# Modulation weights as the moving side, four 32-column tiles at a time, in a two-layer block chain

## The reference, cut to what matters

```python
def ada_mod(cond, w, b, n):
    m = jax.nn.silu(cond) @ w[:, :n * D_MODEL] + b[:n * D_MODEL]
    return m.reshape(m.shape[:-1] + (n, D_MODEL))
...
    for l in range(DEPTH):
        ml = ada_mod(c, w_ada[l], b_ada[l], N_MOD)[:, None]
        mc = ada_mod(c_ctx, w_ada[l], b_ada[l], 2 if last else N_MOD)

        hl = modulate(x, ml[..., 0, :], ml[..., 1, :])
        hc = modulate(ctx, mc[0], mc[1])
        zl = hl @ w_in[l] + b_in[l]
...
        x = layer_norm(DEEPNORM_ALPHA * x + ml[..., 2, :] * mix(zl, attn_l), ln1_g[l], ln1_b[l])

        x = layer_norm(DEEPNORM_ALPHA * x + ml[..., 5, :] * ffn(modulate(x, ml[..., 3, :], ml[..., 4, :])),
                       ln2_g[l], ln2_b[l])
```

## Time and profile before

| | us |
|---|---|
| median of 3 runs | 3683.21 |
| lowest, highest | 3680.97, 3690.7 |
| profiled execution | 3681.75 |
| its span, first to last instruction | 3680.0 |

### The profile page before, as it was taken

One profiled execution on the slowest core, in us unless ns is written; L12 is line 12 of the kernel. 1 busy time (PEld: TensorE's weight loads), 2 busy tenths in 40 slices (PEclk: granted clock), 3 DMA queues, 4 the chain that ended last, 5 costly groups with the idle time before them and its releaser, 6 DMA issues.

```text
span 3680.0 us, 46744 instructions
## 1 busy us (share of the span) xinstructions
PE 3446.7 (94%) x17080; PEld 2772.8 (75%) x17080; DVE 1949.7 (53%) x2633; ACT 1258.7 (34%) x1750; POOL 848.1 (23%) x336
## 2 busy tenths in 40 slices
PE   8999979999979999997999999889997999999997
PEld 8899866787858888875887777678884875677665
DVE  2678886622446253446767873474554624244233
ACT  1221235224233222224223534243224345453433
POOL 1000200232213223230012033334442321332211
PEclk9999999999989999998999999999998989999899
DMA  5333100112102111213531023222221210221111
GB/s 209 125 137 120 51 20 8 50 50 78 62 29 69 63 63 62 64 57 115 173 107 46 7 74 104 85 74 92 96 94 59 69 52 29 75 86 46 63 35 58
DMA packets 72807, 272.00 MB, mean 74 GB/s; under 512 B 8528, under 2 KB 9040, under 8 KB 71888
## 3 DMA queue, kind: packets, MB, share of 16 engines
q1 hardware_dynamic: 71216, 256.04, 21.2%
q10 hardware_dynamic: 1440, 13.89, 1.0%
HBM read 264.66 MB, written 5.24 MB: 73 GB/s over the span
## 4 chain that ended last, share of the span: by engine, by line
PE 86%; DVE 6%; ACT 3%; issue 2%; DVEq 1%; ACTq 1%; DMA 1%; SPq 0%
PE ps L497 47%; PE ps L733 10%; PE ps L589 5%; PE ps L467 4%; PE ps L504 3%; PE ps L567 2%; PE ps L682 2%; PE ps L869 1%; PE ps L555 1%; PE ps L846 1%; PE ps L704 1%; PE ps L967 1%; PE ps L948 1%; PE ps L840 1%; PE ps L964 1%
## 5 line engine op out<-in xcount | busy, mean ns | idle before, releaser
L429 POOL TENSOR_TENSOR w_lo<-w_raw,w_hi 128x1024 fp32r<-128x1024 f32 x332 | 847.9, 2556 | 2792.5 <-ACT w_hi L1064 2792.4
L497 PE MATMUL ps<-act_hi,w_hi 128*128 128x512 f32 x2656 | 570.9, 363 | 9.3 <-DVE arena L2016 2.0
L497 PE MATMUL ps<-act_lo,w_hi 128*128 128x512 f32 x2656 | 560.9, 357 | 0.0
L497 PE MATMUL ps<-act_hi,w_lo 128*128 128x512 f32 x2656 | 547.4, 354 | 0.0
L497 PEld LDWEIGHTS ps<-act_hi,w_hi 128*128 128x128 f32 x2656 | 440.9, 190 | 96.8 <-issue 22.4
L1064 ACT ACTIVATE w_hi<-w_raw 128x1024 fp32r<-128x1024 f32 x380 | 399.8, 1054 | 294.0 <-PE ps L497 89.7
L497 PEld LDWEIGHTS ps<-act_hi,w_lo 128*128 128x128 f32 x2656 | 434.7, 188 | 72.0
L497 PEld LDWEIGHTS ps<-act_lo,w_hi 128*128 128x128 f32 x2656 | 433.0, 188 | 67.8
L1858 DVE SCALAR_TENSOR_TENSOR x<-arena,vec,x 128x512 f32<-128x512 f32 x336 | 220.2, 684 | 0.0
L1850 DVE SCALAR_TENSOR_TENSOR arena<-arena,vec 128x783 f32<-128x783 f32 (+1 forms) x240 | 219.8, 916 | 0.0
L589 PEld LDWEIGHTS ps<-cond,arena 128*128 128x128 f32 x1152 | 163.4, 217 | 18.2 <-issue 11.1
(11 more groups left out here) (309 smaller groups left out, 4967.4 us busy)
## 6 DMA issues: line engine op xcount, KB each, us to landing
w_raw<-in_weights SPq DMA_DIRECT2D x380, 512.0 KB, 3.4
arena<-in_ada_w SPq DMA_DIRECT2D x72, 512.0 KB, 4.5
tmp<-in_ada_w SPq DMA_DIRECT2D x24, 512.0 KB, 4.9
x<-in_x SPq DMA_DIRECT2D x1, 3072.0 KB, 13.6
x<-in_x ACTq DMA_DIRECT2D x1, 3072.0 KB, 9.9
x_mid<-x ACTq DMA_DIRECT2D x1, 3072.0 KB, 9.7
x<-x_mid ACTq DMA_DIRECT2D x1, 3072.0 KB, 10.0
arena<-in_pool_w ACTq DMA_DIRECT2D x2, 1024.0 KB, 5.0
```

Source lines behind the costliest of these rows:

```text
L429: nc.gpsimd.tensor_tensor(WL[:, w], raw, WH[:, w].bitcast(f32), ALU.subtract).then_inc(units_split, 1)
L497: last = nc.tensor.matmul(ps(t, a, b), w[:, s * UNIT + k * P:s * UNIT + (k + 1) * P], act[:, k * TOK + a:k * TOK + b], start=(n == 0 and k ...
```

## The change

The two sides of the modulation matmul are exchanged. The condition, after Silu, is written 16 times over into the space of `gla_w` (32 columns per chunk: 16 copies of 2), and is the stationary side; the weights move past it, 512 columns at a time. A step takes one chunk of 128 contracted channels and 2048 outputs (two slots of 512 KB) and is four matmuls, each writing another 32 partitions of one PSUM bank. Eight steps make the sums of two modulation vectors for both conditions, so the 96 units are 48 steps in 6 groups. A group's sums lie as rows: ACT copies them to the arena (`ada_copy`), and four float32 matmuls against columns of the identity turn them back into the columns that `modulation` reads (`ada_turned`).

- The first 8 steps have arena space of their own for 12 of their 16 loads, so SP issues all 16 without a wait; `x` comes behind them, in two halves. PE waits for `loaded`, the second half of `x` included, ahead of the first `ada_turned`.
- The other 40 steps stand ahead of whole units (`ada_ahead`), never in `first_pair` and no longer between the products of a unit: two ahead of the third unit of layer 0 and one ahead of each later one up to the end of `gate0`; in layer 1 one ahead of every second unit of `conv`, then one ahead of each, and two at the end.
- The loops of PE and ACT over these stages are written out. SP loads `gla_w` behind the last step.
- `TAPS_AT`, layer 0: per pair of units 14 -> 10, per gate 8 -> 6, per key head 3, per query head 3 -> 6, behind all heads 20 -> 10, per tile 1. Layer 1: 11 -> 8, 7 -> 5, key 1 -> 2, query 1 -> 5, behind 25 -> 14, per tile 2. The rest in `gate2` now stands ahead of the wait for the gate's tile.

```diff
-TAPS_AT = ((14, 8, 3, 20, 1), (11, 7, 1, 25, 2))
+TAPS_AT = ((10, 6, 3, 6, 10, 1), (8, 5, 2, 5, 14, 2))
...
-    STAGES += [((_l, "ada_rest"), 0, (0, 0, 0, 1)), ((_l, "conv"), 4, (8, 8, 0, 0)), ((_l, "gate0"), 2, (4, 4, 0, 0)),
+    STAGES += [((_l, "ada_rest"), 0, (0, 0, 1, 1)), ((_l, "conv"), 4, (8, 8, 0, 0)), ((_l, "gate0"), 2, (4, 4, 0, 0)),
...
-ADA_LATER = ((0, "conv", 4, (1, 0, 1)), (0, "gate0", 2, (1, 0, 1)), (1, "conv", 4, (0, 0, 1)), (1, "gate0", 2, (0, 1, 1)))
+ADA_LATER = ((0, "conv", 4, 2), (0, "gate0", 2, 2), (1, "conv", 4, 1), (1, "gate0", 2, 2))
+ADA_STEPS = CH
+ADA_AT = ({u: (0, 1) if u == 2 else (u - 1,) for u in range(2, 3 * CH + 1)},
+          {**{2 * i + 3: (24 + i,) for i in range(CH)}, **{u: (14 + u,) for u in range(18, 24)}, 24: (38, 39)})
+ADA_TURNED = ({9: 1, 17: 2, 25: 3}, {18: 4, 25: 5})
...
+            for i in range(ADA_FIRST // 2):
+                ada_early_load(i)
+            for dst, src in ((VEC1T, vec1_d), (IDENT, consts_d[0]), (PERM, consts_d[1]), (ONES, consts_d[2])):
                 sp.dma_start(dst[:, :], src).then_inc(loaded, 16)
             sp.dma_start(RC[:, :], consts_d[3][:, 0:64]).then_inc(loaded, 16)
+            for i in range(ADA_FIRST // 2, ADA_FIRST):
+                ada_early_load(i)
             for s in range(2):
                 sp.dma_start(RAW[:, s * UNIT:(s + 1) * UNIT], weights[s]).then_inc(raw_landed[s], 16)
-            with sp.Fori(1, ADA_FIRST // ADA_SLOTS) as r:
-                for s in range(ADA_SLOTS):
-                    sp.wait_ge(on(0, "ada_used"), r * ADA_SLOTS + (s - ADA_SLOTS + 1))
-                    ada_load(r * ADA_SLOTS + s, s)
+            for k, landed in enumerate((x_half, loaded)):
+                part = slice(k * CH // 2 * TOK, (k + 1) * CH // 2 * TOK)
+                sp.dma_start(X[:, part], x_d[:, part]).then_inc(landed, 16)
...
                 def single(i, s):
+                    if ahead:
+                        ahead(i * SLOTS + s)
                     start(i, s)
...
-            def ada_chunk(col, slot, k):
-                last = nc.tensor.matmul(at(PS, col + ADA_PS, 2), ada_slot(slot, k * P, P), COND[:, 2 * k:2 * k + 2],
-                                        start=(k == 0), stop=(k == CH - 1))
...
+            def ada_step(p, k, parts):
+
+                for m, src in enumerate(parts):
+                    for half in range(2):
+                        j = 2 * m + half
+                        last = nc.tensor.matmul(ada_sums(p, slice(32 * j, 32 * j + 32)),
+                                                GLA_W[:, 32 * k:32 * k + 32],
+                                                src[:, half * 512:half * 512 + 512], start=(k == 0), stop=(k == CH - 1))
+                last.then_inc(on(0, "ada_used"), 1)
+
+            def ada_turned(p):
+
+                pe.wait_ge(on(0, "ada_copied"), p + 1)
+                a = ADA_PS + mod(p // 3, p % 3 * 2, 0, 0)
+                for q in range(4):
+                    last = nc.tensor.matmul(PS[:, a:a + 4 * CH].rearrange("p (j q r) -> p q j r", j=4, q=4)[:, q:q + 1]
+                                            .rearrange("p q j r -> p (q j) r"),
+                                            AR[:, ADA_ROWS + q * P:ADA_ROWS + (q + 1) * P],
+                                            IDENT[:, :].rearrange("p (j x) -> p j x", j=4)[:, :, 0:2], start=True, stop=True)
+                last.then_inc(on(0, "ada_image"), 1)
...
                 if l == 0:
 
                     pe.wait_ge(*at_least(0, "cond", 1))
+                    pe.wait_ge(tile_free[2], taken(0, "ada_rest", 2, 0))
+                    for k in range(CH):
+                        pe.wait_ge(ada_landed[k // 2], 64)
+                        ada_step(0, k, [ada_early(2 * k), ada_early(2 * k + 1)])
+                    pe.wait_ge(loaded, 6 * 16)
                     pe.wait_ge(tile_free[3], taken(0, "ada", 3, 0))
+                    ada_turned(0)
...
+            def ada_copy(p, last):
+                act.wait_ge(on(0, "ada_used"), ADA_STEPS * (p + 1))
+                if p:
+                    act.wait_ge(on(0, "ada_image"), p)
+                i_ = nc.scalar.activation(AR[:, ADA_ROWS:ADA_ROWS + 512], ada_sums(p), ACT.Copy)
```

More of the change, by code:

```diff
@@ L389, in _ @@
                 sp.dma_start(INVF[:, :], consts_d[3][:, 64:65]).then_inc(tables_loaded, 16)
-            first = ADA_FIRST
-            for l, st, rounds, each in ADA_LATER:
-                n = sum(each)
+            first = 0
+            for l, st, rounds, n in ADA_LATER:
                 if l and st == "conv":
@@ L484, in linear @@
                                 single(j + 1, s)
+                elif ahead:
+                    for i in range(rounds):
+                        for s in range(SLOTS):
+                            single(i, s)
                 else:
@@ new lines, in block1 @@
+                    for c in range(CH):
+                        if c == CH // 2:
+                            act.wait_ge(loaded, 6 * 16)
+                        for j, (a, b) in enumerate(BOTH):
+                            last = nc.scalar.activation(XH[:, c * TOK + a:c * TOK + b], X[:, c * TOK + a:c * TOK + b], ACT.Identity,
+                                                        bias=at(MOD, mod(0, 0, c, j), 1), scale=at(MOD, mod(0, 1, c, j), 1))
+                        last.then_inc(on(l, "h_hi"), 1)
@@ L1230, in block1 @@
+                for j in range(CH):
+                    act.wait_ge(*at_least(l, "glu", j + 1))
+                    evacuate_unit(l, "gate0", j // SLOTS, j % SLOTS, AR[:, B0 + j * TOK:B0 + j * TOK + W], ACT.Sigmoid, B_MERGE)
+                    ada_behind(2 * CH + j)
                 act.wait_ge(*at_least(l, "qk_bias", 1))
```

143 lines of the change are left out of this document (68 added, 75 removed).

## The result

| | before | after |
|---|---|---|
| median | 3682.09 us (4 runs) | 3559.87 us (4 runs) |
| lowest, highest | 3677.12, 3690.7 | 3555.82, 3562.77 |
| profiled execution | 3681.75 | 3559.22 |
| its span | 3680.0 | 3557.4 |

A forecast was written before the change was run, and what follows sets the result against it. PE, holding 86% of the chain, was taken as the bound. Terms -35.6 (start and first pair), -42.4 and -35.1 (units), +0.9 (turn) and +2 (taps) gave -110: from 3681.75 to 3572 us, range 3555 to 3625.

The forecast's parts named there:

- Price of a step: One modulation step on PE: 0.85 us streaming plus 0.44 for entering and leaving tiled form, 1.3 us against 3.4.
- The row I went by: Profiled burst of 16 float32 matmuls on four 64 x 64 tiles, costing 1.29 us, taken as a step's price.
- a sharing of lanes: Rival, chance 0.19: column tiles share, a step takes 2.15 to 2.56 us, total 3606 to 3622 us.
- a line: Rival, chance 0.07: column tiles run one after another, a step takes 3.85 us, total 3702 us, slower.
- The start: Opening modulation, eight steps: loads and x set the time, first activation at 38 instead of 64.54 us, 26.5 earlier.
- First pair: First pair of layer 0, no modulation between products: 24.3 us instead of 33.4, 9.1 less.
- I let it cover three chunks again: First pair, layer 0: PE's slow pace lasts three chunks of 4.0 us, then five take 2.17 each.
- 22 units, layer 0: Layer 0 units behind the first pair, with 24 steps: 220.7 us instead of 263.16, -42.4.
- 22 units, layer 1: Layer 1 units behind the first pair, with 16 steps: 144.0 us instead of 179.07, -35.1.
- Feeders: Units of both layers: DVE, ACT and loads keep up at no cost; late-feeder rival 3597 to 3612 us, chance 0.10.
- Taps moved: Conv taps moved between heads ahead of attention, both layers: +2 us, between -3 and +8; PE's 17.81 wait stays.
- Sum: Whole kernel: all terms together -110 us, from the profiled 3681.75 to 3572 us.

The follow-up runs named there:

- the double step: Changed kernel with each of the 40 later modulation steps issuing its four matmuls twice in a row into the same sums: 3595.49 us.
- turn_early: Changed kernel with the second half of x on its own semaphore, so PE turns the first sums without waiting for all of x: 3549.63 us.
- before_early: Kernel before with the first 16 modulation units' loads issued up front into own space, x behind them, matmuls unchanged: 3676.48 us beside 3682.09.

## Why the prediction was right, point by point

- **Price of a step** (1.3 us, bounds 1.2 and 3.85): right mechanism, 0.1 too dear. The three forms in which only the side by side was changed gave 3.3, 2.08 and 1.2 us for one, two and four tiles, and the double step split 1.21 into 0.85 and 0.36; I had 0.85 and 0.44. The row I went by, a burst on 64 x 64 tiles, was nearest in kind and slightly dearer. Neither a sharing of lanes nor a line was seen. By the ratio that the Trainium skill ("TensorE: Matmul & The Clock Gate", Part 3) has for three tiles, carried to four, I had estimated 1.5. Here the trace does not agree: the runs gave 0.85 of streaming, four of four.
- **The start** (first activation at 38, -26.5): it came at 40.11, -24.4. PE's wait there was ended by `x`, as I said; but `x` was there at 37.50 instead of 35. The term was mis-sized by 2.1 us, within the 3 that I gave it, and turn_early shows that the wait for it was no need. The first six of the eight steps ran at the slow pace, as I said, the last two at the fast one (26.27 to 28.19); that cost and gave nothing under the wait for `x`. What I read in the profile there, a granted clock of 1.00, was no reading (see below), so going by the lengths was right.
- **First pair** (24.3 us): 21.9. The step that failed is "I let it cover three chunks again": the slow pace ended within the first (44.25). The other seven went at PE's own 2.1 us each, with one wait of 1.76 for the DVE, a term that I had at nothing. That the third unit's step came at 61.99, where I had 62, is in part luck: a start 2.1 late and a pair 2.4 short.
- **22 units, layer 0** (-42.4): -46.7. 24 steps at 0.1 us less are 2.4, and the slow stretch of 1.4 that I had put at its head is not there.
- **22 units, layer 1** (-35.1): -38.8, of which the step gives 1.3 and the two steps that stand together at the end 0.35. Of the slow stretch of 1.6 a third is left (its first row takes 2.63 us at 1627.05; 2.11 is usual, 3.39 was before). About a microsecond stays unaccounted for.
- **Feeders** ("no cost, if the DVE keeps up"): right. PE was busy for 215.97 of 216.51 us. One load was late, by 0.54 us, ahead of the second step at 63.59, where I had it hidden.
- **Taps moved** (+2): between 278.50 and 423.06 the stretch was 0.9 us longer, with the turn that I had counted apart (+0.9) in it; in layer 1 3.1 us longer. Together 4.0, against 2.9 for the two terms. The waits were another pair than I said: "PE's wait of 17.81 ahead of attention stays" was wrong by its place. It is 12.08 there and 3.03 ahead of a swap, since the filled DVE held up a head; the sum and the end of it stayed.
- **Sum**: -110 forecast, -122.6 in the traces. Of the 12.6 between them, 0.4 come from the start and the first pair together, 4.3 and 3.7 from the units of the two layers, 1.1 go the other way at the taps, and 1.6 and 3.6 were won between the attention of layer 0 and the third unit of layer 1, and behind the attention of layer 1, where the diff touches nothing that is late. These 5.2 us I can claim in no term.

They lie within what two executions of one kernel differ by. The changed kernel and the one with the old taps show where such differences sit. From the third score of layer 0 they run alike to the microsecond up to 962; then this row in the changed kernel and its twin, with the windows around them (length, busy PE, clock, DMA share, GB/s), first of the changed kernel, then with the old taps:

```profile
956.00:966.00 10.00, 6.89 (x27) 0.83 0.06 7
...
962.71 4.48 PE L523 MATMUL ps<-arena,ones 128*128 128x512 f32 x8 [3.11 <-ACT arena L1130]
```
```profile
956.00:966.00 10.00, 6.89 (x33) 1.00 0.06 7
...
962.53 2.85 PE L523 MATMUL ps<-arena,ones 128*128 128x512 f32 x8 [3.11 <-ACT arena L1130]
```

The same row takes 4.48 us in the one and 2.85 in the other, where the granted clock is 0.83 and 1.00, and PE had waited 3.11 us just before in both. This one place moved the rest of the execution by 1.6 us. I did not trace the 3.6 us further, so their cause stays open.

## What to carry to other kernels

Where a matmul has a handful of columns against a large matrix, let the matrix move and the few columns stand, and fill the array with column tiles: here 32 records of 3.4 us became 1.2, of which 0.85 is streaming, so do two such steps together when their loads allow it. Without the tiles the same step took 3.3, so in this kernel the exchange by itself paid at the start only. When that shortens PE's stage, the filler work of another engine has to be dealt out anew, and it goes where that engine idles under a busy PE, not where PE waits for it: a wait whose releaser has filler queued ahead of it is a wait for the filler (17.81 to 2.44 us here). A wait for a group of loads that stands in a short chain is worth splitting by what the next instruction really reads: for all of `x` it cost 6 us in the changed kernel, for four loads instead of one 3.7 in before_early.
